# A transformer kernel on one core: norm-2 factor from token sums inside the last k step, activation split moved into the last gated slots, last down slot shared by ScalarE and VectorE, latents in PSUM banks 2 to 5

## The reference, cut to what matters

```python
h  = h + rms_norm(mix @ w_out, ln_post_mix)          # norm 1
hn = rms_norm(h, ln_pre_ffn)                         # norm 2
gu = hn @ w_gate_up
ff = (silu(gu[..., :2816]) * gu[..., 2816:]) @ w_down
h  = h + rms_norm(ff, ln_post_ffn)                   # norm 3
# then twice, for each hybrid layer
ada = silu(c) @ w_ada + b_ada                        # shift, scale, gate
u   = x * (1 + scale) + shift
proj = u @ w_in                                      # q_lat 384, kv_lat 256, k_rope 32, c_gate 512, ...
q   = rms_norm_2(q_lat, q_norm_g) @ w_uq
kv  = rms_norm_2(kv_lat, kv_norm_g) @ w_ukv
```

## Time and profile before

| | |
|---|---|
| median of three runs | 2003.44 us |
| profiled execution | 1998.23 us, its span 1996.4 us |
| mean granted TensorE clock | 0.958 |
| TensorE busy | 1818.6 us, 91% |
| VectorE busy | 1068.3 us, 54% |
| ScalarE busy | 703.0 us, 35% |
| GpSimd busy | 129.9 us, 7% |
| chain that ended last | 67% of the span on TensorE, 7% on VectorE, 3% on ScalarE |

### The profile page before, as it was taken

One profiled execution on the slowest core, in us unless ns is written; L12 is line 12 of the kernel. 1 busy time (PEld: TensorE's weight loads), 2 busy tenths in 40 slices (PEclk: granted clock), 3 DMA queues, 4 the chain that ended last, 5 costly groups with the idle time before them and its releaser, 6 DMA issues.

```text
span 1996.4 us, 20299 instructions
## 1 busy us (share of the span) xinstructions
PE 1818.6 (91%) x8139; PEld 1416.4 (71%) x8139; DVE 1068.3 (54%) x1694; ACT 703.0 (35%) x1131; POOL 129.9 (7%) x129
## 2 busy tenths in 40 slices
PE   4999999889999998989999999994889999999993
PEld 3765555568888787767778788773667778788772
DVE  6144444286666325563447867553453448866453
ACT  3324444342221223245532322423255532322422
POOL 1100000101010001000000000013000000000012
PEclk9899999799999999999989999997899999999996
DMA  3311000225555322121113222221121112232210
GB/s 131 131 66 41 22 22 22 74 95 211 180 209 183 114 104 106 63 85 64 64 43 104 86 94 96 85 92 56 64 85 64 64 43 105 85 106 85 98 71 42
DMA packets 29100, 177.40 MB, mean 89 GB/s; under 512 B 3565, under 2 KB 3709, under 8 KB 11726
## 3 DMA queue, kind: packets, MB, share of 16 engines
q1 hardware_dynamic: 20016, 144.71, 20.3%
q0 software_dynamic: 8608, 31.21, 4.6%
q10 hardware_dynamic: 382, 0.19, 0.1%
HBM read 171.28 MB, written 4.78 MB: 88 GB/s over the span
## 4 chain that ended last, share of the span: by engine, by line
PE 67%; DVE 7%; ACT 3%; POOL 1%; issue 1%; DMA 1%; POOLq 0%; ACTq 0%; DVEq 0%
PE ps L553 21%; PE ps L555 20%; PE ps L554 20%; PE ps L1006 2%; DVE w_lo L1462 2%; PE ps L991 2%; DVE R L1507 1%; ACT h L1053 1%; POOL acc L472 1%; ACT w_hi L1053 1%; PE ps L997 1%; PE ps L593 1%; DVE cacc L1469 0%; DMA w_raw<-in_w 0%; DVE ps L1824 0%
## 5 line engine op out<-in xcount | busy, mean ns | idle before, releaser
L553 PE MATMUL ps<-Xh,w_hi 128*128 128x512 f32 x1616 | 652.3, 404 | 55.7 <-DVE Xl L1462 26.2
L555 PE MATMUL ps<-Xh,w_lo 128*128 128x512 f32 x1616 | 636.5, 394 | 0.0
L554 PE MATMUL ps<-Xl,w_hi 128*128 128x512 f32 x1616 | 636.3, 394 | 0.0
L1462 DVE TENSOR_TENSOR w_lo<-w_raw,w_hi 128x2048 fp32r<-128x2048 f32 (+1 forms) x152 | 313.6, 2063 | 339.7 <-ACT w_hi L1053 339.7
L553 PEld LDWEIGHTS ps<-Xh,w_hi 128*128 128x128 f32 x1616 | 308.0, 191 | 132.7 <-issue 42.5
L1053 ACT ACTIVATE w_hi<-w_raw 128x2048 fp32r<-128x2048 f32 (+1 forms) x152 | 259.4, 1707 | 314.4 <-DMA w_raw<-in_w 282.5
L554 PEld LDWEIGHTS ps<-Xl,w_hi 128*128 128x128 f32 x1616 | 308.6, 191 | 65.9 <-issue 4.6
L555 PEld LDWEIGHTS ps<-Xh,w_lo 128*128 128x128 f32 x1616 | 307.7, 190 | 66.2
L1469 DVE SCALAR_TENSOR_TENSOR cacc<-ain,vec,cacc 128x512 f32<-128x512 f32 x240 | 161.9, 746 | 0.0
L1053 ACT ACTIVATE gt<-ps 128x512 f32<-128x512 f32 x48 | 28.2, 597 | 201.2 <-PE ps L555 201.1
L553 PE MATMUL ps<-act_h,w_hi 128*128 128x512 f32 x176 | 70.9, 403 | 4.3 <-DVE act_l L1462 4.3
(11 more groups left out here) (296 smaller groups left out, 2250.0 us busy)
## 6 DMA issues: line engine op xcount, KB each, us to landing
w_raw<-in_w SPq DMA_DIRECT2D x134, 1024.0 KB, 4.8
ada_w<-in_w_ada POOLq DMA_DIRECT2D x48, 512.0 KB, 4.6
bias_scratch<-brow POOLq DMA_DIRECT2D x2, 1312.0 KB, 5.3
h<-in_xT SPq DMA_DIRECT2D x4, 512.0 KB, 6.2
out<-h SPq DMA_DIRECT2D x1, 2048.0 KB, 6.3
bias<-bias_scratch POOLq DMA_DIRECT2D x1, 1024.0 KB, 7.6
bias<-bias_scratch POOLq DMA_DIRECT2D x1, 512.0 KB, 4.9
cact<-in_c POOLq DMA_DIRECT2D x1, 512.0 KB, 6.6
```

The source lines that it names most:

```text
L553: nc.tensor.matmul(o_, whi, xhi, start=start, stop=False)
L554: nc.tensor.matmul(o_, whi, xlo, start=False, stop=False)
L555: return nc.tensor.matmul(o_, wlo, xhi, start=False, stop=stop)
L1462: return nc.vector.tensor_tensor(o_, a_, b_, op)
```

## The change

`w_lo_done` counts quarters of a slot; `split_ready` waits for one. In `two_slots` the second slot's quarters are awaited as k reaches them, the bank base is a parameter, and with `norm=2` the token sums, the root, the diagonal and the spreading go between the matmuls of the last k. Slot 11's first two tiles are computed k by k (`window_step`), two k before `values(63)` and two after it. The splits of the first four `act` tiles go into the last two gated slots, and the first down slot takes its banks in the order 4, 5, 7, 0, 1, 2, 6, 3. Four ada columns go into down slots 2 to 5. In the last down slot ScalarE copies y tiles 0, 2, 4, 6, 7 and VectorE 1, 3, 5 and also adds the squares; the sums go to bank 0 and the factor to bank 1. The latents of each hybrid layer use banks 2, 3, 4, 5, 0, 6, `sums(nsum)` goes behind the first tile of the third slot, and both parts of slot G+4 are made earlier.

```diff
@@ GpSimd
-            add_early_squares(1, 1)
+            add_up(KD, 1, squares(0, KD - 1, KD))
+            pool.wait_ge(sum_full, 2)
+            pool.sem_inc(sq_added, 1)
...
-            add_early_squares(3, 2)
@@ TensorE
+            def split_ready(g, part=3):
+                pe.wait_ge(w_lo_done, 4 * g + part + 1)
...
+            def window_step(k):
+                pe.wait_ge(o_lo, 4 + k + 1)
+                for j in range(2):
+                    if k == 0:
+                        wait_fill(fills, j)
+                    whi, wlo = w(S_OW, k * T + j * P)
+                    last = mm3(bank(j), whi, wlo, oh[4 + k], ol[4 + k], k == 0, k == 3)
+                    if k == 3:
+                        last.then_inc(tile_full, 1)
...
+                if u == UNITS - 1:
+                    split_ready(S_OW)
+                    window_step(0)
+                    window_step(1)
                 values(u)
+            window_step(2)
+            window_step(3)
...
-            def two_slots(g, ready):
-                pe.wait_ge(w_lo_done, g + 2)
+            def two_slots(g, ready, b0, norm=None):
+                split_ready(g)
                 for k in range(KD):
                     pe.wait_ge(lo_done, ready + k + 1)
+                    if norm is not None and k == KD - 1:
+                        token_sums(norm, (norm + 1) * KD, (), B_ST)
                     for i in range(4):
+                        if i == 2:
+                            split_ready(g + 1, k // 2)
+                        if norm is not None and k == KD - 1 and i == 3:
+                            spread(norm, B_O)
...
-            two_slots(S_GU, KD)
-            sums(2, 3 * KD)
+            two_slots(S_GU, KD, 0, norm=2)
...
-                        for j in range(KD):
+                        for j in (4, 5, 7, 0, 1, 2, 6, 3):
+                            if q == 0 and kk == 0:
+                                down_bank(j)
                             last = product(kk, j)
...
-            pe.wait_ge(down_read, 3)
-            token_sums(3, 4 * KD - 2, (KD - 2, KD - 1), 4)
-            pe.wait_ge(down_read, KD - 2)
-            keep_busy(1, bank(B_O), T)
-            spread(2, 5)
-            keep_busy(3, bank(B_O), T)
+            for b in range(2):
+                fills.take(b)
+                wait_fill(fills, b)
+                fills.f[b].n -= 1
+            token_sums(3, 4 * KD - 2, (KD - 2, KD - 1), 0)
+            keep_busy(1, bank(1), T)
+            spread(3, 1)
+            keep_busy(3, bank(0), T)
...
-                two_slots(G, split0)
-                sums(nsum, nadd + 3)
-                pe.wait_ge(w_lo_done, G + 3)
+                two_slots(G, split0, 2)
+                split_ready(G + 2)
...
+                    if j == 0:
+                        sums(nsum, nadd + 3)
@@ ScalarE
-            root(2)
+            token_root(2, B_ST)
+            sc.wait_ge(r_spread, 2)
+            act_(R[:, :], bank(B_O), ACT.Copy).then_inc(r_copied, 1)
...
                 act_(sgate[:, t % 2, :], tmp[:, t % 2, :], ACT.Silu).then_inc(sgate_done, 1)
+                if t >= KF - 2:
+                    down_hi(t - (KF - 2))
...
                 square(bank(j), 3 * KD + j, j)
+                if j in (0, 2, 4):
+                    y_copied = act_(y[:, j, :], bank(j), ACT.Identity, scale=vec1[:, 3 * KD + j:3 * KD + j + 1])
...
-            token_root(3, 4)
+            token_root(3, 0)
+            for j in (KD - 2, KD - 1):
+                act_(y[:, j, :], bank(j), ACT.Identity, scale=...).then_inc(down_read, 1)
...
                     if k == 4:
-                        next_hi(3)
+                        next_hi(L_CG)
+                        next_hi(L_CG + 1)
@@ VectorE
-            slot_lo(S_GU + 2)
-            inv_root(2)
-            ve.wait_ge(cact_done, 1)
+            for part in range(2):
+                slot_lo(S_GU + 2, part)
+            token_roots(2)
+            for part in range(2, 4):
+                slot_lo(S_GU + 2, part)
+            ve.wait_ge(r_copied, 1)
...
+                if t >= KF - 2:
+                    down_lo(t - (KF - 2))
...
+            for j in range(1, KD - 2):
+                ve.wait_ge(sq_ready, 3 * KD + j + 1)
+                if j == 1:
+                    tt(acc[:, :], sq[:, 0, :], sq[:, 1, :], ALU.add).then_inc(sq_added, 2)
+                else:
+                    ve.wait_ge(sq_added, 3 * KD + j)
+                    tt(acc[:, :], acc[:, :], sq[:, j % 2, :], ALU.add).then_inc(sq_added, 1)
+                if j % 2:
+                    y_copied = ts(y[:, j, :], bank(j), vec1[:, 3 * KD + j:3 * KD + j + 1], None, ALU.mult)
...
+            for part in range(2):
+                slot_lo(SLOTS1 + 1, part)
+            token_roots(3)
...
+                if 1 <= j < 3:
+                    slot_lo(SLOTS1 + 1, j + 1)
...
+                next_lo(L_CG + 1)
                 latents(nsum, 0, 3, V_QG)
-                next_lo(L_CG + 1)
```

More of the change, by code:

```diff
@@ L627, in _ @@
             bias_rows(3)
-            pe.wait_ge(w_lo_done, 2)
+            split_ready(1)
             for j in range(2):
@@ L836, in token_sums @@
                 for t in range(NB):
-                    nc.tensor.matmul(bank(b, 1, c0=t), acc[:, t * P:(t + 1) * P], ones[:, 0:1], start=t == 0, stop=False)
+                    last = nc.tensor.matmul(bank(b, 1, c0=t), acc[:, t * P:(t + 1) * P], ones[:, 0:1], start=t == 0,
+                                            stop=not late and t == NB - 1)
                 for i in late:
@@ L884, in _, with down_bank @@
                     last.then_inc(tile_full if j == 0 else slot_done, 1)
-            for b in range(2):
-                wait_fill(fills, b)
+            def down_bank(j):
+                if j in (0, 2):
+                    pe.wait_ge(bank_read[0], fills.f[0].val())
+                if j == 1:
+                    pe.wait_ge(bank_read[1], fills.f[1].val(-1))
+                if j in (6, 3):
+                    pe.wait_ge(bank_read[1], fills.f[1].val())
             def down_slot(q):
                 g = S_DOWN + q
-                pe.wait_ge(w_lo_done, g + 1)
+                split_ready(g)
                 def product(kk, j):
@@ L1262, in _, with down_hi @@
             slot_hi(S_GU + 2)
-            root(2)
+            token_root(2, B_ST)
+            sc.wait_ge(r_spread, 2)
+            act_(R[:, :], bank(B_O), ACT.Copy).then_inc(r_copied, 1)
             sc.wait_ge(c_in, 16)
             act_(cact[:, :], cact[:, :], ACT.Silu).then_inc(cact_done, 1)
+            def down_hi(q):
+                if q >= 2:
+                    sc.wait_ge(slot_done, q + (S_DOWN - 1))
+                for kk in range(2):
+                    act_(act_h[:, 2 * (q % 2) + kk, :], act[:, 2 * q + kk, :], ACT.Copy).then_inc(ah_done, 1)
             f0, f1 = FILL1[0] - KF, FILL1[1] - KF
@@ L1477, in slot_lo @@
                 last = tt(w_lo[:, g % NBUF, c], w_raw[:, g % NBUF, c], w_hi[:, g % NBUF, c], ALU.subtract)
-                if part in (None, 3):
-                    last.then_inc(w_lo_done, 1)
+                last.then_inc(w_lo_done, 4 if part is None else 1)
             def rest(n, k, xh, xl, src=None):
@@ L1706, in ada_column, with down_lo @@
                 nc.vector.tensor_copy(ada[:, t:t + 1], ada_sum[:, par:par + 1]).then_inc(ada_copied, 1)
-            f0, f1 = FILL1[0] - KF, FILL1[1] - KF
+            def down_lo(q):
+                for kk in range(2):
+                    ve.wait_ge(ah_done, 2 * q + kk + 1)
+                    r = 2 * (q % 2) + kk
+                    tt(act_l[:, r, :], act[:, 2 * q + kk, :], act_h[:, r, :], ALU.subtract).then_inc(al_done, 1)
             for t in range(KF):
```

103 lines of the change are left out of this document (47 added, 56 removed).

## The result

The median fell from 2002.85 us (2001.84 to 2005.49, 4 runs) to 1968.12 us (1965.98 to 1970.48, 4 runs): ratio 0.9825, with 95% between 0.9808 and 0.9842. The forecast was 1969 us. The profiled execution of after took 1970.48 us (span 1968.7), 27.75 us less than the one of before, where the sum of the steps said 32.0.

What follows compares the result with a forecast made beforehand. TensorE was taken to carry the time, with only pauses between stages and the slow clock behind them to win. Terms 6.0 + 7.2 + 7.8 + 11.0 + 0 = 32.0 us gave 1966.2 profiled, 1971.4 on the median side; forecast 1969, range 1961 to 1980.

Steps and rivals of the forecast that it cites:

- Norm 2: Before slot 15: restart 3.0 us earlier with a 0.8 us pause, plus 2.96 us of slow clock won; 6.0 us.
- Down: First down slot: act tiles split earlier, restart 4.2 us earlier plus 3.0 us of slow clock; 7.2 us.
- Last down slot: Last down slot and norm 3: dense work resumes 8.8 us earlier, some given back in the loop; 7.8 us.
- Latents: Both hybrid layers: slot G+5 starts earlier, with a new stall before it; 6.2 and 4.75 us, 11.0 together.
- W_out: W_out's 6.11 us pause hangs on a chain that starts when slot 11 is used up; 0, between -1 and +1.
- a mean clock not above 0.965: Whole kernel, profile after: the prediction is wrong if the mean clock doesn't rise above 0.965.
- the clock isn't won back: Rival, 13%: stalls shrink, but each touched place still brings one slow stretch; about 8 us lost, 1977 us.
- The latents give almost nothing: Rival, 12%: the chain ending in slot G+5 gets longer than reckoned; the gain of 11 becomes 4, 1976 us.
- the act split does not open down: Rival, 6%: last gated act tile waits for ScalarE's splits, bank 3 or 6 late; 7.2 becomes 2, 1974 us.
- a lower clock in the gapless stretches: Rival, 3%, slower than before: the chip takes the clock back in longer gapless stretches; 2009 us.

Runs made afterwards that it cites:

- the fillers: The kernel before, with unread matmuls put into the pauses at norm 2 and before the first down slot: 1999.02 us beside 2006.46.
- e1: The kernel after with norm 2 as before, full ones matmul behind the two slots, root and inverse on 128x512: 1975.52 us.
- e2: The kernel after with the splits of all act tiles back in the down slots, new bank order kept: 1970.63 us.
- e4: The kernel after with the first sums of each hybrid layer again between the two slots and the third: 1975.9 us.
- e5: The kernel after with its last four ada columns again behind the last split of the down stage: 1973.21 us.
- e6: The kernel after without W_out's early steps, slot 11 computed tile by tile behind values(63): 1965.78 us.
- e10: The kernel after with GpSimd's loads of c and the first two ada columns behind its norm 1 additions: 1957.5 us.

## Why the prediction was right

The time is 0.9 us from the forecast, and none of the six rows of the table is off by more than 0.8 us. The mechanism holds in the main, but so close a hit is partly luck. The medians differ by 34.7 us, not 32.0, and the forecast stood between two ways of counting, 1966.2 and 1971.4. The place of one pause was wrong, and the latents vary by 1.6 to 2.9 us from one execution to the next. By steps:

- **Norm 2, 6.0 us.** Measured 5.83 from the first dense matmul of slot 13 (the 5.2 of the table holds 0.6 us of slower norm 1), and 5.3 given back when undone. The restart's pause was 0.81 where 0.8 was said, and slot 15 runs in 11.19. The clock part was sized 2.96; the fillers measured 2.65.
- **Down, 7.2 us.** Measured 7.27; no pause, as said.
- **Last down slot, 7.8 us.** Measured 7.61, and 10.57 us from product to dense matmul where 10 was said. Two things in it were off. Norm 3 was to run at clock 1.00; at 784 to 787 it is 0.56, and the spreading takes 1.70 us, not 1.16. And the argument put the gain on shared tiles and moved columns alike, while 6.5 of it belongs to the columns alone.
- **Latents, 11.0 us.** Measured 6.8 + 5.0 = 11.8. Over the six kernels with the same latents it is 5.3 to 8.2 and 5.0 to 6.7 us against the profile of before. The times in it hold well: with E the end of the first two slots (slot 47's end, 813.2), the third slot ends at E + 11.8 (said 11.9), and G+5 starts at E + 38.8 (said 38.4). But the step's statement of where TensorE stands was wrong: "the stall of 4.50 us before G+4 does not vanish, a stall of 3.7 us comes before G+5". The stall stayed before G+4, 2.79 us long, and G+5 had none. The prediction's chain looked for the low part of G+5 as the last thing. It counted ScalarE's two gate SiLUs in that chain, but not that the first of them frees bank 0 for G+4's first tile. The late start of G+4 hid the stall before G+5: with the bank read first that stall appears, 2.20 us long. So G+5's start came out right while the place of the pause did not. Both go only when G+5's parts are made ahead of latents 3 and 4 as well.
- **W_out, 0.** Measured +0.46 to slot 12's end, and the pause is 6.18 us. The early k were to cover some tenths; slot 11 ends 0.85 us later instead, and up to slot 13's first dense matmul it is +1.09 us, which lies just outside the stated -1 to +1.

The prediction named a mean clock not above 0.965 as a sign against it. It was 0.963 in the profiled execution of after. That sign was badly chosen: the mean also holds the start, where from 43 to 50 us instructions that didn't change ran at 0.55 in this execution, and at 1.00 in that of the kernel without W_out's early steps. The stretches behind the touched pauses are the test, and there the clock did rise, except in part of norm 3 and behind the new latent pause. It fell where nothing was expected, in norm 1.

Of the rivals, "the clock isn't won back" (listed first, called the second where the rule is weighed) happened in a small part: 0.80 at 840 to 846 and 0.56 at 784 to 787. The Trainium skill ("TensorE: Matmul & The Clock Gate", section "HAM oscillation — how this bites in real kernels") says that bursts broken by waits can pay for the low clock again each time. The runs agree with "can". The same pause of 2.79 us stands in both layers of seven profiles (after, e1, e2, e4, e5, e6, e10), and slots 48 to 50 or 92 to 94 took 27.05 to 28.56 us in eight of these fourteen passages and 25.66 to 25.70 in six. "The latents give almost nothing" and "the act split does not open down" didn't happen, and neither did a lower clock in the gapless stretches.

Between the median and the profiles: 34.7 us of difference in medians, 31.44 in the touched segments, 27.75 in the two profiled executions. The 3.7 us between the last two is clock at the start and elsewhere. The profile of after was the slowest of its four runs and that of before lay below all its timed runs, which narrows the difference between the two by the rest.

## What to carry to other kernels

The pauses of 4 to 5 us at norm 2 and before down cost their length and 1.8 to 3.0 us of slow clock behind it, so price both; and work that merely fills idle room (here four column reductions worth 6.5 us, and GpSimd's wait for a slot with the DMA issues behind it, worth 8.2 us) belongs anywhere but ahead of a norm. Where a stall is expected to move, list for every engine what it has queued ahead of each PSUM read that frees a bank, and not only what the next operand needs: an instruction that frees a bank goes ahead of those that wait for long chains. Work pulled forward to cover a wait can cost more than it covers (the early steps of W_out, 1.1 us), so undo each part once on its own. Judge a step by its own segment of the stream, since a mean clock or a whole time carries noise from places that the change doesn't touch.

## What the runs showed of the hardware

The start of the kernel isn't reproducible. With the same instructions in the same order, slot 1 ends anywhere from 71.8 to 77.0 us over the profiled executions, and the clock from 43 to 50 us was 0.53 to 1.00. No run tells what decides it.

VectorE and GpSimd hold each other up. The low part of a slot takes 2.29 us alone; before, it took 3.94 at 856.71, since GpSimd's copy of 3.60 us had begun at 854.91 and ended 1.80 us later:

```profile
854.91 3.60 POOL L530 COPY K<-krope 64x4096 f32<-64x4096 f32 x1 [13.78 <-ACT krope L1053]
856.71 3.94 DVE L1462 TENSOR_TENSOR w_lo<-w_raw,w_hi 128x2048 fp32r<-128x2048 f32 x1 [1.90 <-ACT w_hi L1053]
```

This low part is the one that TensorE waited for before slot G+4, so 1.65 of the 4.50 us of that pause came from the copy. Made early, it takes 2.29 us at 827.62 in the kernel after, ahead of the copy at 837.62. With the order turned round (the run with the banks read first), the low part that began at 835.65 takes 2.28 and the copy 5.57 instead of 3.59:

```profile
835.65 2.28 DVE L1508 TENSOR_TENSOR w_lo<-w_raw,w_hi 128x2048 fp32r<-128x2048 f32 x1
835.83 5.57 POOL L527 COPY K<-krope 64x4096 f32<-64x4096 f32 x1 [13.54 <-ACT krope L1087]
```

The one that comes second pays about the whole overlap (1.65 of 1.80 us, 1.98 of 2.10). The Trainium skill ("SBUF — State Buffer", section "Terms") says that the two engines share a port pair that is locked for a full instruction, and that the loser blocks; these two cases agree.
